# VectorE gathers the forward states of the outputs stage; the odd projection's first operands are asked for in the output gate

## The reference, cut to what matters

```python
a_bar = jnp.exp(a * dt)                       # one complex number for each group and state
_, states = lax.associative_scan(_linear_combine, (a_seq, bu), axis=1, reverse=reverse)
y = y + jnp.einsum('blgn,gpn->blgp', states, c).real.reshape(bsz, l, S5_WIDTH)
y = jax.nn.gelu(y)
```

```python
o = jax.nn.sigmoid(xc @ w_ogate + b_ogate)
hh = (o * cell + skip * xc) * silu(z)
return hh @ w_out
```

## Time and profile before

| | |
|---|---|
| median of three runs | 2729.38 us (2726.0 to 2730.17) |
| the profiled execution | 2730.53 us, of which the span of the profile is 2728.4 us |
| PE busy | 2500.1 us, 92% of the span |
| outputs stage | from 862 us to about 1001 us of the span |
| end of the output gate, start of the odd projection | 2525 us to 2558 us of the span |

### The profile page before, as it was taken

How to read it: one execution, slowest core, us unless ns; L and a number is a source line. 1 busy time by engine, 2 the same in 40 slices (tenths; PEclk the granted TensorE clock), 3 DMA queues, 4 the chain that set the end, 5 groups by cost and what they waited for, 6 DMA issues and landing times. The chain is left out here.

```text
span 2728.4 us, 40576 instructions
## 1 busy us (share of the span) xinstructions
PE 2500.1 (92%) x15206; PEld 2163.2 (79%) x15206; DVE 1403.9 (51%) x2104; ACT 1003.8 (37%) x2146; POOL 1129.5 (41%) x1114
## 2 busy tenths in 40 slices
PE   6999998789998769899799999899898799999798
PEld 5988887678886669677688888787776699999687
DVE  6559887667775235415555444555555442222314
ACT  4232222766674331323232223365565420000331
POOL 3445442067774236320245354343343255554320
PEclk9999999989999989999899999899999899999899
DMA  6424443301113664535323334443434264442544
GB/s 165 106 77 144 137 140 117 110 26 48 40 39 114 164 159 152 183 113 160 98 105 131 124 120 148 149 151 129 153 105 168 73 240 147 141 141 94 194 161 154
DMA packets 271015, 349.27 MB, mean 128 GB/s; under 512 B 45652, under 2 KB 212206, under 8 KB 268406
## 3 DMA queue, kind: packets, MB, share of 16 engines
q1 hardware_dynamic: 226902, 268.59, 31.5%
q10 hardware_dynamic: 43936, 78.26, 8.1%
HBM read 223.23 MB, written 114.03 MB: 124 GB/s over the span
## 5 line engine op out<-in xcount | busy, mean ns | idle before, releaser
L1105 POOL TENSOR_TENSOR w_hi<-w_raw,ones 128x512 fp32r<-128x512 f32 (+1 forms) x232 | 290.9, 1254 | 760.2 <-PE r L1116 329.1
L1116 PE MATMUL r<-h_lo,w_hi 128*128 128x264 f32 (+1 forms) x1200 | 395.7, 330 | 7.4 <-PEq L2543 7.4
L1116 PE MATMUL r<-h_hi,w_lo 128*128 128x264 f32 (+1 forms) x1200 | 387.4, 323 | 0.0
L1116 PE MATMUL r<-h_hi,w_hi 128*128 128x264 f32 (+1 forms) x1200 | 386.6, 322 | 0.0
L1107 POOL TENSOR_TENSOR w_lo<-w_raw,w_hi 128x512 fp32r<-128x512 f32 (+1 forms) x232 | 351.2, 1514 | 18.2
L1116 PEld LDWEIGHTS r<-h_lo,w_hi 128*128 128x128 f32 x1200 | 227.3, 189 | 28.9 <-issue 9.9
L1116 PEld LDWEIGHTS r<-h_hi,w_hi 128*128 128x128 f32 x1200 | 227.3, 189 | 21.3 <-issue 2.4
L1116 PEld LDWEIGHTS r<-h_hi,w_lo 128*128 128x128 f32 x1200 | 227.3, 189 | 17.6
L1846 PE MATMUL o<-v,prob 116*116 116x129 f32 (+1 forms) x1296 | 166.1, 274 | 0.3 <-ACT prob L1896 0.3
L1116 PE MATMUL x<-h_lo,w_hi 128*128 128x264 f32 (+1 forms) x432 | 156.1, 361 | 6.9 <-POOL w_lo L1107 6.9
L1846 PEld LDWEIGHTS o<-v,prob 116*116 116x116 f32 (+1 forms) x1296 | 158.4, 180 | 3.9 <-ACT prob L1896 0.5
(11 more groups left out here) (384 smaller groups left out, 6251.2 us busy)
## 6 DMA issues: line engine op xcount, KB each, us to landing
w_raw<-in_w_in_even SPq DMA_DIRECT2D x72, 256.0 KB, 3.3
w_raw<-in_w_in_odd SPq DMA_DIRECT2D x64, 256.0 KB, 3.5
w_raw<-in_w_ogate SPq DMA_DIRECT2D x64, 256.0 KB, 2.8
v_d<-vs ACTq DMA_DIRECT2D x8, 1152.0 KB, 4.2
us<-u_d SPq DMA_DIRECT2D x16, 520.0 KB, 5.1
xc_d<-xc ACTq DMA_DIRECT2D x8, 1040.0 KB, 6.5
qk_d<-qk ACTq DMA_DIRECT2D x16, 520.0 KB, 2.7
qk<-qk_d SPq DMA_DIRECT2D x8, 1040.0 KB, 5.0
```

The lines of the kernel that those rows point to most:

```text
L1105: self.nc.gpsimd.tensor_tensor(hi, raw, one, ALU.mult).then_inc(self.hi_done, 1)
L1116: ins = self.nc.tensor.matmul(bank[:, 0:n], w[:, u % self.buffers, k, :], z[:, off:off + n], start=(first and k == 0 and w is self.hi and ...
```

## The change

It has two independent parts, and a third edit that only serves the second.

1. In the outputs stage the gather of the forward states goes from ACT to DVE. DVE's order becomes: gather 0, then for each n: lags(n), set_b_apart(n + 2), and behind it gather 1 (n = 0), nothing (n = 1 and 2), gathers 2 and 3 (n = 3), gather n (n = 4 to 7). ACT keeps windows, evicts and stores.
2. In the output gate, at the end of SP's list, behind the last operands of the gate, SP asks for row blocks 0 and 1 of `w_out_odd` and, when six of the `hh` tiles are stored, for the first six operand tiles of the odd projection (three transfers of two tiles each). They go to `room`. `project_rows` asks only for the fourth pair of tiles itself.
3. `x_raw` becomes a list of tiles of two, so that three of them can lie in `room` and one in a tile of its own. The even layer's transfers stay as they were.

```diff
-                for n in range(1, NB):
+                def gather(n):
                     if n >= 2:
-                        set_b_apart(n)
-                    lags(n - 1)
-                lags(NB - 1)
+                        dve.wait_ge(done, (n - 1) * GB)
+                    for q in range(2):
+                        ins = v.tensor_copy(rhs[f, n % 2, :, q, :],
+                                            t["Z"][f, 0:CH, q, n * GB:(n + 1) * GB].rearrange("p c g -> p g c"))
+                    ins.then_inc(gathered[0], 1)
+
+                gather(0)
+                for n in range(NB):
+                    lags(n)
+                    if n + 2 < NB:
+                        set_b_apart(n + 2)
+                    for m in {0: (1,), 1: (), 2: (), 3: (2, 3)}.get(n, (n,)):
+                        gather(m)
...
-                gather(0)
-                gather(1)
                 act.wait_ge(lag_copied, 2)
...
                 for n in range(NB):
                     evict(n)
-                    if n + 2 < NB:
-                        gather(n + 2)
...
-            ogate(nc, a, c, d, h, weights, len(units), sz0)
-        below.close()
-        project_rows(nc, a, d, c, a["w_out_odd"], d["hh"], 1, LAST_ROWS, out=out)
+            given = dict(w=given["w"], x=[room[:, 2 * D + q * 768:2 * D + (q + 1) * 768] for q in range(3)],
...
+            ogate(nc, a, c, d, h, weights, len(units), sz0, given)
+        project_rows(nc, a, d, c, a["w_out_odd"], d["hh"], 1, LAST_ROWS, out=out, given=given)
...
+                w_out = a["w_out_odd"].rearrange("(k p) n -> k p n", p=P)
+                hh = d["hh"].rearrange("k p t -> p k t")
+                sp.wait_ge(made, 4)
+                for b in range(2):
+                    sp.dma_start(given["w"][:, b, :], w_out[b]).then_inc(given["w_loaded"][b], 16)
+                for b in range(2):
+                    sp.wait_ge(stored[b], 16 * 3)
+                for q in range(3):
+                    sp.dma_start(given["x"][q], hh[:, 2 * q:2 * q + 2, META:META + 3 * P]).then_inc(given["x_loaded"][q], 16)
...
-                if not given:
-                    load_w(0)
-                    load_x(0, 0, 0)
-                    load_w(1)
-                    for q in range(1, NQ):
-                        load_x(0, 0, q)
+                for q in range(len(given["x"]), NQ):
+                    load_x(0, 0, q)
```

More of the change, by code:

```diff
@@ L126, in trunk @@
         given = dict(w=room[:, 0:2 * D].rearrange("p (b n) -> p b n", b=2),
-                     x=room[:, 2 * D:].rearrange("p (k m) -> p k m", k=KC),
+                     x=[room[:, 2 * D + q * 2 * FIRST_COLS:2 * D + (q + 1) * 2 * FIRST_COLS].rearrange(
+                         "p (k m) -> p k m", k=2) for q in range(4)],
                      w_loaded=[low.sem(f"w_loaded{b}") for b in range(2)],
@@ L164, in trunk @@
             mlstm_z(nc, a, c, d, h, weights, units[count:], count, hs, raw, sz0)
-            ogate(nc, a, c, d, h, weights, len(units), sz0)
-        below.close()
-        project_rows(nc, a, d, c, a["w_out_odd"], d["hh"], 1, LAST_ROWS, out=out)
+            given = dict(w=given["w"], x=[room[:, 2 * D + q * 768:2 * D + (q + 1) * 768] for q in range(3)],
+                         w_loaded=[low.sem(f"w_loaded{b}") for b in range(2)],
+                         x_loaded=[low.sem(f"x_loaded{b}") for b in range(4)])
+            given["x"] = [x.rearrange("p (k m) -> p k m", k=2) for x in given["x"]]
+            ogate(nc, a, c, d, h, weights, len(units), sz0, given)
+        project_rows(nc, a, d, c, a["w_out_odd"], d["hh"], 1, LAST_ROWS, out=out, given=given)
 class Stage:
@@ L341, in load_rows, with project_rows @@
     return 16
-def project_rows(nc, a, d, c, w_out, cat, layer, tiles, out=None, h=None, given=None):
+def project_rows(nc, a, d, c, w_out, cat, layer, tiles, given, out=None, h=None):
     HK, SL, HQ = KC, 3, 2
@@ L356, in project_rows @@
         w = [s.sb(n, [P, HK, D], F32R) for n in ("w_hi", "w_lo")]
-        wr = given["w"] if given else s.sb("w_raw", [P, 2, D])
-        xr = given["x"] if given else s.sb("x_raw", [P, HK, W])
+        wr = given["w"]
+        xr = given["x"] + [s.sb("x_raw", [P, HQ, W]) for q in range(len(given["x"]), NQ)]
         part, early = s.sb("part", [P, 2, D]), s.sb("early", [P, 2, D])
@@ L365, in project_rows @@
         turn = s.ps("turn", 1024)
-        wl = given["w_loaded"] if given else [s.sem(f"w_loaded{b}") for b in range(2)]
+        wl = given["w_loaded"]
         wh_done, wl_done, w_used = s.sem("w_hi_done"), s.sem("w_lo_done"), s.sem("w_used")
-        xl = given["x_loaded"] if given else [s.sem(f"x_loaded{b}") for b in range(NQ)]
+        xl = given["x_loaded"]
         xh_done, xl_done = s.sem("x_hi_done"), s.sem("x_lo_done")
@@ L396, in load_x @@
                         sp.wait_ge(xl_done, HK * at)
[L397 removed]
+                    sp.dma_start(xr[q][:, :, 0:n],
                                  cv[:, hf * HK + q * HQ:hf * HK + (q + 1) * HQ, off:off + n]).then_inc(xl[q], 16)
@@ L551, in x_hi @@
                                 act.wait_ge(summed, min((g + 1) * SL, NTL))
-                        nc.scalar.activation(x[0][:, k, off:off + n], xr[:, k, 0:n], ACT.Copy).then_inc(xh_done, 1)
+                        nc.scalar.activation(x[0][:, k, off:off + n], xr[k // HQ][:, k % HQ, 0:n], ACT.Copy).then_inc(xh_done, 1)
                 def part_copy(t):
@@ L622, in _ @@
                             dve.wait_ge(xh_done, (hf * NG + g) * HK + k + 1)
-                            v.tensor_tensor(x[1][:, k, off:off + n], xr[:, k, 0:n],
+                            v.tensor_tensor(x[1][:, k, off:off + n], xr[k // HQ][:, k % HQ, 0:n],
                                             x[0][:, k, off:off + n].bitcast(F32), ALU.subtract).then_inc(xl_done, 1)
@@ L1038, in _ @@
             def _(act):
[L1039 to L1047, removed]
                 def evict(n):
@@ L2042, in _ @@
                     k = slice(q * KC // 4, (q + 1) * KC // 4)
-                    sp.dma_start(given["x"][:, k, :], cat[:, k, 0:FIRST_COLS]).then_inc(given["x_loaded"][q], 16)
+                    sp.dma_start(given["x"][q], cat[:, k, 0:FIRST_COLS]).then_inc(given["x_loaded"][q], 16)
             @block.gpsimd
@@ L3046, in _, with ogate @@
                             low(k - 1)
-def ogate(nc, a, c, d, h, weights, first, sz0):
+def ogate(nc, a, c, d, h, weights, first, sz0, given):
     NP, NO, SLOTS = len(PIECES), 2 * KC, 8
```

## The result

| | before | with the change |
|---|---|---|
| median of four runs | 2729.78 us (2726.0 to 2730.25) | 2712.14 us (2708.83 to 2713.46) |
| ratio to before, 95% interval | 1 | 0.9933 (0.992 to 0.9947) |
| profiled execution | 2730.53 us, span 2728.4 | 2708.83 us, span 2707.0 |

The kernel became 17.6 us faster by the medians; 19.0 was forecast, with a range of 10.4 to 24.8. The profiled execution happens to be the quickest of the four, so its span is 21.4 us shorter. I therefore cut each span in three at instructions that both kernels have: the outputs stage (from DVE's memset of `b_apart` to the next stage's first `y_hi`), the end (from DVE's last product of `hh` to the end of the span), and the unchanged stages between.

What follows compares the result with a forecast made beforehand. PE, busy 92% of the span, was taken as the bound, so only its idle places pay: outputs stage 13.7 plus odd projection 5.3 makes 19.0 us, from 2729.38 to 2710.4 us; range 2704.6 to 2719.0.

Steps and rivals of the forecast that it cites:

- ACT's gather stands on PE's path, and only until the next thing is late: Outputs stage: each ACT gather costs at most 3.79 us where PE waits for ACT; removing them gains 13.7 us.
- The table is late next: Outputs stage: lags(4) to lags(7) wait for tables, landing 14.8 us after the end of the mix two blocks earlier.
- M(2): End of mix(2) in the outputs stage, forecast at 925.1 with the change.
- Lags and mix together are 11.45 us: Outputs stage, PE per block: a lags takes 6.09 us and eight groups of mix 5.36.
- the sixth table: Outputs stage: the table lags(6) needs, forecast to land at 939.9, 14.8 us after the end of mix(2).
- The gather takes 1.3 us: One DVE gather copy: 1.3 us, twice the dense copy, bounds 0.68 and 3.2; nothing late at the opening.
- Rival 1: DVE gather copy takes 2.3 us: PE 4.1 us late at the opening, gain 14.9, 2714.5 us; chance 0.2.
- DVE and POOL take turns: Outputs stage: DVE's and POOL's copies alternate, a pair of each taking 6.5 us; in the loop this costs nothing.
- Rival 4: Slower than before: DVE and POOL shut each other out at the opening, beyond 6.0 us a copy; chance 0.04.
- Rival 2: Outputs stage: transfers become the bound, tables land 2 us later, gain 13, 2716.4 us; chance 0.17.
- Rival 3: PE stays at full clock in mix(1), mix(6) and mix(7) after shorter stalls: gain 23.3, 2706.1 us; chance 0.12.
- The odd projection, 5.3 us: ACT's first copy runs with the stage's start, 5.3 us earlier, and all of it lasts to the end; bounds 4.5 and 6.

Runs made afterwards that it cites:

- gather twice: The changed kernel with DVE's gathers 0 and 1 done twice each, the same values again: ratio 0.9965 to the kernel before.
- tables first: The changed kernel, but SP asks for table n+2 ahead of the windows and inputs of block n: ratio 0.9904 to the kernel before, 2699.63 us.
- gather only: The kernel before with only the changed outputs stage (gather on DVE), odd projection as before: ratio 0.9963 to the kernel before.

## Why the prediction was right

The sign and both mechanisms held, and the total came within the range; the gain forecast for the outputs stage was too large by 3 us in the profile of the change. Step by step:

- **ACT's gather stands on PE's path, and only until the next thing is late.** Right. Of some 23 us of gathers the stage gained 10.6 to 12.4. The wait before mix(1)'s fifth group is 4.68 us (forecast 4.6), that of mix(6) 2.77, and mix(2) to mix(5) wait for ACT no more.
- **The table is late next.** Right, and the experiment that moves the tables shows it. lags(4) started at 914.01; 913.6 was forecast, and this profile's stage began 0.4 later. lags(6) started 15.2 us after M(2) instead of 14.8. lags(5) and lags(7) did not wait at all, because the blocks before them ended late.
- **Lags and mix together are 11.45 us.** This is the term that was mis-sized. A block took 11.65 where nothing held it (3 and 5): the eight groups of a mix take 5.56 us to the next lags, not 5.36. Blocks 2 and 4 came behind a table's wait and took 1.3 us more each, because PE fell to the lower clock in them. I had kept the lower clock behind the stalls that stood in the trace of before, and put none behind the new stalls that I forecast. These 2.6 us are most of the 3.1 between 13.7 and 10.6, but not all of the account: the longer blocks, the sixth table (0.4 late) and block 6 (11.0 us instead of 10.7) cost another 1.6 or so together, 0.8 came back where lags(7) was to wait for its table and did not, and 0.3 in block 7. The trace of before had a warning that I overlooked, a stall of only 1.83 us in mix(4) with slow groups behind it (PE's timeline there):

```profile
954.50 0.49 PE L1012 MATMUL yp<-us,toe 128*128 128x130 f32 x2 [1.83 <-ACT v L1056]
...
956.08 0.64 PE L1012 MATMUL yp<-us,toe 128*128 128x130 f32 x2
```

- **The gather takes 1.3 us.** It takes less: 2.01 us for the pair at 876.92, with POOL idle, 1.0 each. With POOL beside it a pair takes 3.8 (1.9 each), and 5.39 at the opening:

```profile
866.81 5.39 DVE L976 COPY rhs<-Z 64x1040 f32<-64x1040 f32 x2
872.23 0.62 DVE L967 COPY kt<-lags 16x448 f32<-16x448 f32 x1
...
876.92 2.01 DVE L976 COPY rhs<-Z 64x1040 f32<-64x1040 f32 x2
```

  The first copies of `kt` started 0.3 us later against the stage's start than before, and PE waited for none. Rival 1 (2.3 us) falls. A copy whose reads lie 512 bytes apart took 1.0 us, the dense one 0.68; ACT's factor of 1.8, from which I had taken my 1.3 us, was too much for it. The Trainium skill, SBUF — State Buffer, section Door 1: The DMA port swizzle, says that each access that crosses to a new 16-byte line pays a penalty. The trace agrees as far as these two rows go.
- **DVE and POOL take turns.** Right: POOL's pair went from 3.85 to 5.56 us, by 1.7, which is nearly the 2.0 of DVE's pair. The Trainium skill, SBUF — State Buffer, section Who interferes with whom, says that a VectorE copy in its two-port mode and a GpSimd instruction exclude each other for the whole of the instruction that began first. The trace agrees with these times. Rival 4, the slower side, needed 6 us a copy; gather twice shows the mechanism to be real: 5.4 us more on DVE ahead of the first `kt` made the stage 7.4 us longer.
- **Rival 2, transfers as the bound.** It falls with tables first: 11.7 us a block at a share of 0.91.
- **Rival 3, full clock.** It did not come about for mix(1) (the stall of 4.68 us was followed by slow groups too), nor for mix(6) behind 2.77 us. For mix(7) it came in some executions. In the changed kernel a stall of 1.88 us was followed by slow groups, in gather only one of 1.47 by none:

```profile
983.04 0.49 PE L1022 MATMUL yp<-us,toe 128*128 128x130 f32 x2 [1.88 <-ACT v L1056]
...
984.05 0.64 PE L1022 MATMUL yp<-us,toe 128*128 128x130 f32 x2
```

```profile
983.53 0.49 PE L1022 MATMUL yp<-us,toe 128*128 128x130 f32 x2 [1.47 <-ACT v L1056]
...
984.31 0.39 PE L1022 MATMUL yp<-us,toe 128*128 128x130 f32 x2
```

  From the stores of block 6 to those of block 7 it is 9.6 us in the one and 7.8 in the other, while both ask for the stores of block 6 at 115.4 us of the stage. That is the whole difference between their stages (128.5 and 126.6). Which of the two an execution gets is not explained here; the forecast's excess of 3.1 us would have been 1.3 in the profile of gather only.
- **The odd projection, 5.3 us.** Right within its bounds of 4.5 to 6: 5.3 in the profile of the change, 4.7 alone and on the average of all profiles. That it moves whole is a little too much; some 0.6 us are taken back.

## What to carry to other kernels

When work leaves an engine that another waits for, walk the loop forward once more with the next late thing in its place. Here that was a transfer which was late only by its position in a queue, and asking for it ahead of less urgent ones shortened the stage by another 8 us, but only after the change. Price every new stall of the matrix unit with the slow stretch that may come behind it, too.

## What the runs showed that was not expected

A VectorE copy of 64x1040 float values 512 bytes apart takes 1.0 us, about half of ScalarE's 1.90 and GpSimd's 1.95 for the same pattern. A table of 1 MB landed in 5.4 to 5.9 us when asked for ahead of the eight small windows, against 7.0 to 7.6 behind them. The DMA share from asking to landing of the two loads shown above was 0.97 in both cases, so the engines were as full behind the windows as ahead of them; that the table shared them with the windows' bytes when it stood behind is my reading, which no run separates:

```profile
934.60:942.20 7.60, 4.07 (x37) 3.88 (x35) 4.02 (x4) 1.95 (x7) 3.47 (x2) 1.00 0.97 319
```

```profile
935.50:941.40 5.90, 5.90 (x65) 4.27 (x64) 5.15 (x5) 0.28 (x1) 5.57 (x2) 1.00 0.97 318
```

And the length of a short stall of PE did not settle the clock behind it: stalls of 1.83 and 2.26 us were followed by slow groups, stalls of 2.10 us in the kernel before (mix(2)) and 1.47 us in gather only by none.
